# The upper levels of a block-triangular inverse: products of 128x128 against products of its 64x64 squares

## The chip, the cores and the metric

The kernel runs on one core of a Trainium2 chip. Its time is the device time of one execution, in microseconds (us). A core has TensorE for matrix products (PE in the profile, PEld for its weight loads), VectorE (DVE), ScalarE (ACT), GpSimd (POOL) and SyncE (SP, which issues the DMAs here). SBUF and PSUM have 128 partitions each; TensorE reads SBUF and writes PSUM.

## The reference, cut to what matters

Two blocks of a network work on 256 tokens of width 2048 in float32. The part in question is the gated delta rule of the second block. It runs for eight heads, in two directions, over chunks of 64 tokens:

```python
a_mat = m + jnp.eye(CHUNK)        # m: strictly lower triangular, one per head, direction and chunk
rhs = jnp.concatenate([v * beta, kb * jnp.exp(gc)[..., None]], axis=-1)
sol = lax.linalg.triangular_solve(a_mat, rhs, left_side=True, lower=True, unit_diagonal=True)
...
v_new = uc - jnp.einsum("bhck,bhkv->bhcv", wc, s)
o = jnp.einsum("bhck,bhkv->bhcv", qd, s) + jnp.einsum("bhij,bhjv->bhiv", qkc, v_new)
s = s * gl[..., None, None] + jnp.einsum("bhck,bhcv->bhkv", kd, v_new)
```

The kernel uses chunks of 128 instead of 64, which gives the same sequence of states, and forms the inverse of each 128x128 triangular matrix itself.

## The kernel before, in words

Everything beside the delta rule is mostly large linear layers. Their weights come in units of 128x1024 numbers: a DMA into one of four slots of `raw`, a rounded copy `w_hi` by ACT (L610 in this stage), the rest `w_lo` by POOL (L582), then sixteen matmuls by PE (`product`, L1941 and L1944). A slot is free again when PE has used its unit.

In the delta rule, PE works on one pair of heads at a time, `one_way` (way A below) and `other` (way B), over `PAIRS` = 4 pairs. Each pair's steps are written out by hand in one order for PE, one for ACT and one for DVE, with units of the gates' layer (`fill(n)`, 28 units a pair) put between them where PE would otherwise wait. Way A has PSUM banks `x_ps` and `y_ps` 0 and 1, way B banks 2 and 3. A way holds four matrices (two directions by two chunks), each 128x128, side by side on the free axis: `t` is the inverse so far, `u` its transpose, `m` the triangular matrix.

The inverse is built from diagonal blocks. DVE makes the inverses of the 16x16 blocks by substitution. Three levels then join neighbours: level 4 joins 16 to 32, level 5 joins 32 to 64, level 6 joins 64 to 128. After level 4 or 5, a matrix holds only the diagonal blocks of that size, so its two off-diagonal 64x64 squares are zeros until level 6. A level of a way takes these steps:

- PE, first product: `x_ps = m^T t` for the four matrices (L2385; at level 4 with the masked `mm4`).
- ACT copies `x_ps` to `x` in SBUF (`level` of ACT, L1007).
- PE, second product: `x_ps = u^T x` (L2391, levels 4 and 5 only) and `y_ps = x^T u` (L2392).
- DVE subtracts the result from `t` and `u` (L1732 at level 4, L1744 at level 5, L1751 at level 6, there only the one 64x64 square that is not zero).

PE's order in a level is: first product of A, first of B, second of A, second of B. No `fill` stands between the start of level 4 and the end of `first_solve` (L2398), which needs level 6's result. DVE has one other instruction among these, `group_out` between level 4 and level 5 (L1614, a reduction for the gates' layer). ACT's `fill(23)` (L610) stands right before its first copy. A float32 matmul of the program shows in the trace as two weight loads and two MATMUL records.

Of the kernel before, what the change touches and what calls it, by code (L numbers as in the profile page):

```python
# [20 lines left out]
ALU = mybir.AluOpType  # L21
# [4 lines left out]
P = 128  # L26
# [122 lines left out]
def four1(v):  # L149

    return v.rearrange("p (n i) -> p n i", n=4)


def flat(v):

    return v.rearrange("p d c h -> p (d c h)")
# [40 lines left out]
def build(nc, t, out):  # L197
    ctx = ExitStack()
    with ctx:
# [8 lines left out]
        def steps(name, names):  # L208
            return Steps(sem(name), names)

        def rounds(name, names):
# [117 lines left out]
        dn_dve = [steps(f"dn_dve{w}", ["one"] + [f"cv{y}{k}" for k in range(NT) for y in range(3)]  # L329
                        + ["rn", "rq", "qs", "ks", "dsub", "dmin", "m0", "m1", "m2", "m3", "qk", "blk", "mm4", "red", "dl", "r0", "r1"]  # L330
                        + [y for n in range(1, BASE) for y in (f"pr{n}", f"su{n}")] + ["cp", "ex0", "ex1", "t4", "u4"]
                        + [f"l5{n}" for n in range(4)] + ["u60", "u61", "vd0", "vd1", "v10", "v11", "ra", "rb", "v20", "v21",
                                                          "o", "orn", "on", "ot", "lo"]) for w in range(2)]
# [779 lines left out]
        def _(dve):  # L1113
# [102 lines left out]
            for i in range(4):  # L1216
# [6 lines left out]
                w = ROWS["even_w_dw"]  # L1223
# [409 lines left out]
            for p in range(PAIRS):  # L1633
                def from_pe(w, name):
                    dve.wait_ge(dn_pe[w.w].sem, dn_pe[w.w].at(name, p))
# [92 lines left out]

                def level4(w):
                    from_pe(w, "tu4")  # L1730
                    for part, bank in ((w.t, w.x_ps), (w.u, w.y_ps)):
                        nc.vector.tensor_tensor(part, part, four1(bank), ALU.subtract).then_inc(dn_dve[w.w].sem, 1)  # L1732

                def level5(w):

# [85 lines left out]
                for w in ways:  # L1821
                    level4(w)
# [11 lines left out]
            with dve.Fori(0, 4) as i:  # L1834
                for k in range(2):
# [9 lines left out]
                    fr, part = both[1][:, :, 1, :], scr[:, 2 + k].rearrange("p (m n) -> p m n", m=2)  # L1845
# [49 lines left out]
        def _(pe):  # L1895
# [113 lines left out]
            for q in range(TT):  # L2009
                for c in range(8):  # L2010
                    m = nc.tensor.transpose(ps[:, 2 * q + c // 4, (c % 4) * P:(c % 4 + 1) * P], z[:, Z_AGT + c, q * P:(q + 1) * P], ident[:])
            m.then_inc(ln_pe.sem, 1)
            for j in range(8):
                if j == 5:

                    pe.wait_ge(ln_dve.sem, ln_dve.at("n11"))
                    for c in range(8):
                        for q in range(TT):
                            m = nc.tensor.transpose(ps[:, c // 2, (c % 2) * T + q * P:(c % 2) * T + (q + 1) * P],
                                                    scr[:, 2 * q + c // 4, (c % 4) * P:(c % 4 + 1) * P], ident[:])  # L2020
# [69 lines left out]
            for name, width in (("cq", QL), ("kv", KVW)):  # L2090
                bank = 2 * (OG[name] % 2)
# [25 lines left out]
            for c in range(4):  # L2117
                for q in range(TT):
                    m = nc.tensor.transpose(ps[:, c // 2, (c % 2) * T + q * P:(c % 2) * T + (q + 1) * P], cqn[q][:, c * P:(c + 1) * P], ident[:])
            m.then_inc(od_pe.sem, 1)  # L2120
            pe.wait_ge(od_dve.sem, od_dve.at("kv1"))
            for c in range(2):
                for q in range(TT):
                    m = nc.tensor.transpose(ps[:, 2, c * T + q * P:c * T + (q + 1) * P], ckvn[q][:, c * P:(c + 1) * P], ident[:])
            m.then_inc(od_pe.sem, 1)
            for q in range(TT):
                m = nc.tensor.transpose(ps[:, 3, q * P:(q + 1) * P], ikn[:, q * P:(q + 1) * P], ident[:])
# [153 lines left out]
            for c in range(DC):  # L2281
                m = nc.tensor.matmul(ps[0:64, 0, :], sc_w[:, c].rearrange("p h n -> p (h n)"), a[:, c].rearrange("p s n -> p (s n)"), start=(c == 0), stop=(c == DC - 1))
# [10 lines left out]
            for q in range(TT):  # L2293
                for s in range(2):
                    m = nc.tensor.matmul(ps[:, 1, q * 32:q * 32 + 32], sc_feat[:, s * T + q * P:s * T + (q + 1) * P], pick,
                                         start=(s == 0), stop=(s == 1))
            m.then_inc(sc_pe.sem, 1)
            pe.wait_ge(group_free, IN2_G + 4)
            for g in range(FG):
                if g:  # L2300
                    pe.wait_ge(fo_act.sem, fo_act.at("ab", g - 1))
                for q in range(TT):
                    m = nc.tensor.matmul(ps[:, 2, q * T:(q + 1) * T], z[:, Z_F + g, q * P:(q + 1) * P], z[:, 40, :], start=True, stop=True)
# [5 lines left out]
                for q in range(TT):  # L2309
                    for s in range(2):  # L2310
                        m = nc.tensor.matmul(ps[:, 3, 0:T], z[:, 48 + q, s * P:(s + 1) * P], z[:, 41 + 2 * s + q, :],  # L2311
                                             start=(q == 0 and s == 0), stop=(q == 1 and s == 1))
# [3 lines left out]
                if g == 3:  # L2316
                    pe.wait_ge(sc_dve.sem, sc_dve.at("g1"))
                    for n in range(4):
                        d = n % 2
                        m = nc.tensor.matmul(ps[:, 0, 16 * n:16 * n + 16], tri[:, n, :], flat(dsc[:, GG])[:, 16 * d:16 * d + 16], start=True, stop=True)  # L2320
                    m.then_inc(sc_pe.sem, 1)
            blk = lambda v, n: v[:, n * P:(n + 1) * P]
            for p in range(PAIRS):
# [4 lines left out]
                def from_act(w, name):  # L2328
                    pe.wait_ge(dn_act[w.w].sem, dn_act[w.w].at(name, p))

                def from_dve(w, name):
                    pe.wait_ge(dn_dve[w.w].sem, dn_dve[w.w].at(name, p))
# [39 lines left out]
                def turn(w):  # L2372
# [2 lines left out]
                        m = nc.tensor.transpose(blk(w.y_ps, n), w.tu[:, at, :], ident[:])  # L2375
                    m.then_inc(dn_pe[w.w].sem, 1)

                def level(l, ready):
                    for w in ways:
                        if l == 4:  # L2380
                            from_act(w, "tt")
                        else:
                            from_dve(w, ready)
                        for n in range(4):
                            m = nc.tensor.matmul(blk(w.x_ps, n), (w.mm4 if l == 4 else w.m)[:, n, :], w.t[:, n, :], start=True, stop=True)  # L2385
                        m.then_inc(dn_pe[w.w].sem, 1)
                    for w in ways:
                        from_act(w, f"x{l}")
                        for n in range(4):
                            if l < 6:  # L2390
                                nc.tensor.matmul(blk(w.x_ps, n), w.u[:, n, :], w.x[:, n, :], start=True, stop=True)  # L2391
                            m = nc.tensor.matmul(blk(w.y_ps, n), w.x[:, n, :], w.u[:, n, :], start=True, stop=True)  # L2392
                        m.then_inc(dn_pe[w.w].sem, 1)

                def first_solve(w):
# [61 lines left out]
                for l, ready in ((4, None), (5, "u4"), (6, "l53")):  # L2457
                    level(l, ready)
# [79 lines left out]
```

## Time and profile before

| what | value |
|---|---|
| median of 3 runs | 2274.88 us (2274.41 to 2275.27) |
| profiled execution | 2274.89 us, span 2273.1 us |
| PE busy | 98% of the span |
| DVE, ACT, POOL busy | 45%, 46%, 75% |
| levels 4 to 6, each of the four pairs | 16.0 us of the span |

A busy share is the time in which an engine had at least one instruction under way. Matmuls are pipelined: one starts before the last has drained, so PE's pace is read from the starts of its rows, not from the length of one. In a timeline row, neighbouring instructions of one line and kind are merged, with their number behind the x.

### The profile page before, as it was taken

The numbers are of one execution on the slowest core, as the hardware profiler recorded it, in microseconds if no ns is written. First come the engines' busy times: TensorE is split into PE (matmuls) and PEld (weight loads), VectorE is DVE, ScalarE is ACT, GpSimd is POOL, SyncE is SP. The second block draws the span as 40 slices with busy tenths as digits, with TensorE's granted clock in tenths as the row PEclk, the third lists the DMA queues.
The fourth block names the chain that finished last, engine by engine and source line by source line (L and its number), as shares of the span: only waits on it lengthen the run. The fifth ranks groups of instructions, "written<-read, shape, count | busy, mean of one in ns | idle before, by whom it ended". The sixth has DMA issues, their size and how long they took to land.

```text
span 2273.1 us, 33387 instructions
## 1 busy us (share of the span) xinstructions
PE 2217.1 (98%) x12170; PEld 1909.5 (84%) x12170; DVE 1027.0 (45%) x1762; ACT 1036.3 (46%) x1442; POOL 1715.4 (75%) x721
## 2 busy tenths in 40 slices
PE   7999999999999999999999999999999999999998
PEld 6888888878888788888888888887888888888886
DVE  3991242025853141647473734405813822831841
ACT  5433455454566554535353535444333333333343
POOL 6888868867667975657474747897888888888885
PEclk9999999999999999999999999999999999999999
DMA  6666545646445654535353535665666656656654
GB/s 208 189 191 189 182 139 176 195 124 178 145 140 190 213 150 125 146 109 158 106 156 110 158 107 175 198 204 156 188 194 192 188 194 190 190 193 191 190 191 142
DMA packets 321435, 384.05 MB, mean 169 GB/s; under 512 B 14654, under 2 KB 255141, under 8 KB 321061
## 3 DMA queue, kind: packets, MB, share of 16 engines
q1 hardware_dynamic: 317237, 376.75, 54.8%
q10 hardware_dynamic: 4080, 5.64, 0.8%
q8 instruction: 85, 1.39, 0.3%
q14 instruction: 33, 0.27, 0.0%
HBM read 380.24 MB, written 2.10 MB: 168 GB/s over the span
## 4 chain that ended last, share of the span: by engine, by line
PE 92%; DVE 2%; issue 2%; ACT 2%; POOL 1%; DMA 1%; ACTq 0%; POOLq 0%; DVEq 0%
PE lin_ps L1941 35%; PE lin_ps L1944 17%; PE lin_ps L1982 9%; PE lin_ps L1980 9%; PE lin_ps L1981 9%; POOL w_lo L582 1%; PE ps L2392 1%; PE ps L1913 1%; PE ps L2385 1%; PE ps L2391 1%; PE ps L2311 1%; ACT w_hi L610 1%; PE ps L2243 0%; DMA raw<-in_odd_w_out 0%; PE lin_ps L2166 0%
## 5 line engine op out<-in xcount | busy, mean ns | idle before, releaser
L582 POOL TENSOR_TENSOR w_lo<-raw,w_hi 128x1024 fp32r<-128x1024 f32 x716 | 1715.1, 2403 | 538.6 <-ACT w_hi L610 440.4
L1941 PE MATMUL lin_ps<-a,w_hi 128*128 128x512 f32 x3200 | 1020.9, 400 | 0.9 <-POOL w_lo L582 0.8
L610 ACT ACTIVATE w_hi<-raw 128x1024 fp32r<-128x1024 f32 x456 | 479.2, 1059 | 568.8 <-PE lin_ps L1944 356.1
L1944 PEld LDWEIGHTS lin_ps<-a,w_lo 128*128 128x128 f32 x3200 | 601.9, 188 | 142.2
L1944 PE MATMUL lin_ps<-a,w_lo 128*128 128x256 f32 x3200 | 629.9, 278 | 0.0
L1941 PEld LDWEIGHTS lin_ps<-a,w_hi 128*128 128x128 f32 x3200 | 491.4, 189 | 8.5 <-issue 5.2
L621 ACT ACTIVATE w_hi<-raw 128x1024 fp32r<-128x1024 f32 x228 | 242.1, 1062 | 384.8 <-PE lin_ps L1944 225.6
L1980 PE MATMUL lin_ps<-w_hi,b 128*128 128x512 f32 x704 | 274.7, 390 | 1.6 <-POOL w_lo L582 1.5
L1981 PE MATMUL lin_ps<-w_lo,b 128*128 128x512 f32 x704 | 274.0, 389 | 0.0
L1982 PE MATMUL lin_ps<-w_hi,b 128*128 128x512 f32 x704 | 273.9, 389 | 0.0
L1980 PEld LDWEIGHTS lin_ps<-w_hi,b 128*128 128x128 f32 x704 | 132.1, 188 | 30.2 <-POOL w_lo L582 3.0
L1981 PEld LDWEIGHTS lin_ps<-w_lo,b 128*128 128x128 f32 x704 | 132.2, 188 | 27.3
L1982 PEld LDWEIGHTS lin_ps<-w_hi,b 128*128 128x128 f32 x704 | 132.1, 188 | 27.3
L1179 DVE SCALAR_TENSOR_TENSOR x<-x,lin_ps 128x512 f32<-128x512 f32 x32 | 20.6, 683 | 296.5 <-PE lin_ps L1982 296.5
L1941 PE MATMUL lin_ps<-b,w_hi 128*128 128x512 f32 x352 | 112.5, 401 | 2.9 <-POOL w_lo L582 2.2
L1980 PE MATMUL lin_ps<-w_hi,a 128*128 128x512 f32 x256 | 99.8, 390 | 0.0
L1982 PE MATMUL lin_ps<-w_hi,a 128*128 128x512 f32 x256 | 99.6, 389 | 0.0
L1981 PE MATMUL lin_ps<-w_lo,a 128*128 128x512 f32 x256 | 99.6, 389 | 0.0
L1880 DVE TENSOR_TENSOR b<-scr,b 128x512 f32 x32 | 92.4, 2889 | 4.7 <-DVE b L1878 0.5
L1876 DVE SCALAR_TENSOR_TENSOR scr<-scr 128x512 f32<-128x512 f32 x32 | 88.8, 2775 | 1.1
L1238 DVE SCALAR_TENSOR_TENSOR ps<-z,vec,ps 128x254 f32<-128x254 f32 (+28 forms) x232 | 88.2, 460 | 0.0
L1878 DVE CAST b<-scr 128x512 f32 x32 | 78.0, 2437 | 5.1 <-DVE scr L1876 5.1
(379 smaller groups left out, 2154.6 us busy)
## 6 DMA issues: line engine op xcount, KB each, us to landing
raw<-in_w_in SPq DMA_DIRECT2D x144, 512.0 KB, 3.7
raw<-in_w_mlp_up SPq DMA_DIRECT2D x128, 512.0 KB, 3.9
raw<-in_w_mlp_down SPq DMA_DIRECT2D x128, 512.0 KB, 3.6
raw<-in_even_w_in SPq DMA_DIRECT2D x112, 512.0 KB, 3.6
raw<-in_odd_w_in SPq DMA_DIRECT2D x40, 512.0 KB, 3.7
raw<-in_even_w_out SPq DMA_DIRECT2D x32, 512.0 KB, 4.2
raw<-in_odd_w_out SPq DMA_DIRECT2D x32, 512.0 KB, 4.6
raw<-in_w_o SPq DMA_DIRECT2D x32, 512.0 KB, 4.4
```

Source lines behind the costliest of these rows:

```text
L582: nc.gpsimd.tensor_tensor(w_lo[:, slot], raw[:, slot], w_hi[:, slot].bitcast(F32), ALU.subtract).then_inc(lo_done, 1)
L610: nc.scalar.activation(w_hi[:, slot], raw[:, slot], ACT.Copy).then_inc(hi_done, 1)
L621: nc.scalar.activation(w_hi[:, slot], raw[:, slot], ACT.Copy).then_inc(hi_done, 1)
L1238: nc.vector.scalar_tensor_tensor(out=acc[c][:, k:T], in0=u[c][:, 0:T - k], scalar=per_channel(w + 8 * (TAPS - 1 - k) + c), in1=acc[c][:, k:T],
L1876: nc.vector.scalar_tensor_tensor(out=tm2, in0=tmp, scalar=0.0, in1=tmp, op0=ALU.max, op1=ALU.mult).then_inc(ml_dve.sem, 1)
L1878: nc.vector.tensor_copy(bb[:, :, 0, :], tm2).then_inc(ml_dve.sem, 1)
L1880: nc.vector.tensor_tensor(bb[:, :, 1, :], tm2, bb[:, :, 0, :].bitcast(F32), ALU.subtract).then_inc(ml_dve.sem, 1)
L1941: nc.tensor.matmul(lin_ps[:, 2 * parity + m, :], hi[:, k, m * P:(m + 1) * P], src[:, kk].rearrange("p s n -> p (s n)"), start=(q == 0 and ...
L1944: last = nc.tensor.matmul(lin_ps[:, 2 * parity + m, 0:T], lo[:, k, m * P:(m + 1) * P], src[:, kk, 0, :], start=False, stop=(q == n - 1 and ...
L1980: nc.tensor.matmul(acc, ah, hi[:, k, :], start=(j == 0 and k == 0), stop=False)
L1981: nc.tensor.matmul(acc, ah, lo[:, k, :], start=False, stop=False)
L1982: last = nc.tensor.matmul(acc, al, hi[:, k, :], start=False, stop=(j == 7 and k == 1))
```

## The change

At levels 4 and 5 each product of two 128x128 matrices is written as two products of 64x64 squares, one on partitions 0 to 63 and one on 64 to 127, each writing its own square of PSUM. At level 6 each product is the one 64x64 square that is used: for the first two of the four matrices it goes from partitions 0 to 63 to partitions 64 to 127 in the first product, for the other two the other way round, and back in the second. The off-diagonal squares of levels 4 and 5 are no longer written, so DVE's subtraction of level 4 takes only the diagonal squares, as 64 partitions by 8 by 64, in two instructions as before. ACT's copies are as they were.

```diff
                 def level4(w):
                     from_pe(w, "tu4")
-                    for part, bank in ((w.t, w.x_ps), (w.u, w.y_ps)):
-                        nc.vector.tensor_tensor(part, part, four1(bank), ALU.subtract).then_inc(dn_dve[w.w].sem, 1)
+                    blocks = w.xy_ps.rearrange("p (m n) -> p m n", m=8)
+                    for rows in (slice(0, 64), slice(64, P)):
+                        nc.vector.tensor_tensor(w.tu[rows, :, rows], w.tu[rows, :, rows], blocks[rows, :, rows], ALU.subtract).then_inc(dn_dve[w.w].sem, 1)
...
+                def squares(l, n):
+
+                    halves = slice(0, 64), slice(64, P)
+                    return [(h, h) for h in halves] if l < 6 else [(halves[n // 2], halves[1 - n // 2])]
+
                 def level(l, ready):
                     for w in ways:
...
                         for n in range(4):
-                            m = nc.tensor.matmul(blk(w.x_ps, n), (w.mm4 if l == 4 else w.m)[:, n, :], w.t[:, n, :], start=True, stop=True)
+                            for k, o in squares(l, n):
+                                m = nc.tensor.matmul(w.x_ps[o, P * n + k.start:P * n + k.stop], (w.mm4 if l == 4 else w.m)[k, n, o], w.t[k, n, k],
+                                                     start=True, stop=True)
                         m.then_inc(dn_pe[w.w].sem, 1)
                     for w in ways:
                         from_act(w, f"x{l}")
                         for n in range(4):
                             if l < 6:
-                                nc.tensor.matmul(blk(w.x_ps, n), w.u[:, n, :], w.x[:, n, :], start=True, stop=True)
-                            m = nc.tensor.matmul(blk(w.y_ps, n), w.x[:, n, :], w.u[:, n, :], start=True, stop=True)
+                                for k, o in squares(l, n):
+                                    nc.tensor.matmul(w.x_ps[k, P * n + k.start:P * n + k.stop], w.u[k, n, k], w.x[k, n, k], start=True, stop=True)
+                            for k, o in squares(l, n):
+                                m = nc.tensor.matmul(w.y_ps[k, P * n + o.start:P * n + o.stop], w.x[o, n, k], w.u[o, n, o], start=True, stop=True)
                         m.then_inc(dn_pe[w.w].sem, 1)
```

PE before, first pair, level 4: the first products of way A (tiles in `z`) and way B (`scr`), then the second products of way A. The numbers behind the names are partitions by columns of the moving operand, as the program writes it.

```order
L2385 MATMUL ps<-z 128x128 x4
L2385 MATMUL ps<-scr,z 128x128 x4
L2391 MATMUL ps<-z 128x128
L2392 MATMUL ps<-z 128x128
L2391 MATMUL ps<-z 128x128
L2392 MATMUL ps<-z 128x128
```

The same place in the changed kernel, whose lines 2392, 2400 and 2402 are these three matmuls.

```order
L2392 MATMUL ps<-z 64x64 x8
L2392 MATMUL ps<-scr,z 64x64 x8
L2400 MATMUL ps<-z 64x64 x2
L2402 MATMUL ps<-z 64x64 x2
L2400 MATMUL ps<-z 64x64 x2
L2402 MATMUL ps<-z 64x64 x2
```

Each matmul has become two of half the edge, in the same place between the waits; a way's level goes from 12 matmuls to 24 at levels 4 and 5.

PE before, first pair, level 6 (first products of A and B, then the second ones).

```order
L2385 MATMUL ps<-z 128x128 x4
L2385 MATMUL ps<-scr 128x128 x4
L2392 MATMUL ps<-z 128x128 x4
L2392 MATMUL ps<-scr 128x128 x4
```

The same place in the changed kernel.

```order
L2392 MATMUL ps<-z 64x64 x4
L2392 MATMUL ps<-scr 64x64 x4
L2402 MATMUL ps<-z 64x64 x4
L2402 MATMUL ps<-scr 64x64 x4
```

Here the number stays, and only the size goes down. On DVE two instructions of 64x8x64 a way stand where two of 128x512 stood, and nothing else moves on any engine.

## Rows read from the trace of the kernel before

**Rows 1.** The page, busy time and instructions of each engine

```profile
PE 2217.1 (98%) x12170; PEld 1909.5 (84%) x12170; DVE 1027.0 (45%) x1762; ACT 1036.3 (46%) x1442; POOL 1715.4 (75%) x721
```

**Rows 2.** Windows, levels of pairs 1 and 4: PE, PEld, DVE, ACT, POOL; clock, DMA

```profile
986.80:1002.80 16.00, 15.09 (x131) 14.61 (x129) 6.54 (x15) 4.53 (x7) 3.43 (x2) 1.00 0.29 86
...
1320.90:1336.90 16.00, 15.09 (x131) 14.61 (x130) 6.54 (x15) 4.53 (x7) 3.42 (x2) 1.00 0.28 82
```

**Rows 3.** Timeline of PE, first pair: start, us, line, shapes, number [idle before]

```profile
986.83 1.06 PE L2385 MATMUL ps<-z 128*128 128x128 f32 x8
987.72 1.06 PE L2385 MATMUL ps<-scr,z 128*128 128x128 f32 x8
988.68 0.49 PE L2391 MATMUL ps<-z 128*128 128x128 f32 x2
...
992.36 1.06 PE L2385 MATMUL ps<-z 128*128 128x128 f32 x8
993.90 1.16 PE L2385 MATMUL ps<-scr 128*128 128x128 f32 x8 [0.48 <-DVE scr L1732]
...
998.46 1.06 PE L2385 MATMUL ps<-z 128*128 128x128 f32 x8
999.95 1.16 PE L2385 MATMUL ps<-scr 128*128 128x128 f32 x8 [0.43 <-DVE scr L1744]
...
1002.79 0.62 PE L2398 MATMUL ps<-z 128*128 128x128 f32 x4
1003.65 0.71 PE L2398 MATMUL ps<-z,scr 128*128 128x128 f32 x4 [0.24 <-DVE scr L1751]
```

**Rows 4.** Timeline of ACT, same stretch

```profile
987.08 1.06 ACT L610 ACTIVATE w_hi<-raw 128x1024 fp32r<-128x1024 f32 x1 [1.25 <-PE lin_ps L1944]
988.05 0.58 ACT L1007 ACTIVATE z<-ps 128x512 f32<-128x512 f32 x1
...
993.45 0.60 ACT L1007 ACTIVATE z<-ps 128x512 f32<-128x512 f32 x1 [4.04 <-PE ps L2385]
```

**Rows 5.** Timeline of DVE, same stretch

```profile
992.56 1.28 DVE L1732 TENSOR_TENSOR scr<-scr,ps 128x512 f32<-128x512 f32 x2 [0.50 <-PE ps L2392]
993.76 1.22 DVE L1614 TENSOR_REDUCE z<-lin_ps 128x512 f32<-128x1024 f32 x1
...
998.67 1.23 DVE L1744 TENSOR_TENSOR scr<-scr,ps 32x128 f32<-32x128 f32 x4 [0.56 <-PE ps L2392]
1002.04 0.60 DVE L1751 TENSOR_TENSOR z<-z,ps 64x128 f32<-64x128 f32 x2 [2.14 <-PE ps L2392]
```

**Rows 6.** Timeline of POOL, its first instruction after the same stretch

```profile
1008.47 2.40 POOL L582 TENSOR_TENSOR w_lo<-raw,w_hi 128x1024 fp32r<-128x1024 f32 x1 [17.90 <-ACT w_hi L610]
```

**Rows 7.** Timeline of PE, indexer of the first block, operands on 64 partitions

```profile
545.40 0.39 PE L1944 MATMUL lin_ps<-b,w_lo 128*128 128x256 f32 x2
545.72 0.93 PE L2196 MATMUL ps<-own,z 64*128 64x128 f32 x8
546.58 0.50 PE L1941 MATMUL lin_ps<-b,w_hi 128*128 128x512 f32 x1
...
549.56 0.39 PE L2196 MATMUL ps<-own,z 64*128 64x128 f32 x2
```

**Rows 8.** The line of these matmuls: ns of one, min/median/max, and shapes

```profile
L2196 PE MATMUL ps<-own,z x64: 272/374/378, 541.0 to 569.3; 64*128 64x128 f32 x32, 64*128 64x256 f32 x32
```

**Rows 9.** A line that loads weights of 64 columns: ns of one, min/median/max

```profile
L2282 PEld LDWEIGHTS ps<-a,b x16: 133/134/135, 849.7 to 853.1; 128*64 128x64 f32 x16
```

**Rows 10.** Timeline of PEld, eight weight loads before matmuls of only 16 columns

```profile
890.08 0.98 PEld L2320 LDWEIGHTS ps<-dsc,tri 128*128 128x128 f32 x8
```

**Rows 11.** Windows around PE's idle stretches of 1.05 and 2.17 us

```profile
737.90:741.40 3.50, 2.45 (x12) 1.70 (x10) 0.00 (x0) 1.47 (x2) 2.38 (x1) 1.00 1.11 362
...
1377.80:1381.20 3.40, 1.34 (x7) 1.16 (x8) 2.62 (x3) 2.74 (x4) 3.40 (x2) 1.00 0.01 2
1381.30:1384.60 3.30, 3.30 (x13) 2.82 (x12) 0.69 (x1) 0.42 (x2) 3.30 (x3) 0.50 0.80 241
```

## The prediction

> **What bounds the kernel now.** I read the page first: PE is busy for 98% of the span, no other engine for more than 75% [rows 1], so time is only won where PE's own instructions go or PE's waits shrink. Then the windows of the four stretches in which levels 4 to 6 run: the reader is to see that each is 16 us long with PE busy for 15.1, DVE for 6.5, ACT for 4.5, and that the first and the last pair agree to the hundredth, at a granted clock of 1.00 (2.4 GHz) [rows 2]. I can work out one pair and take it four times. The timeline of PE in the first pair shows the levels as almost one closed run from 986.83 to the start of `first_solve` at 1002.79, broken by two waits for DVE, 0.48 and 0.43 us, and a third of 0.24 before way B's solve at 1003.65 [rows 3]. So this stretch is bound by PE, with DVE close behind. POOL has filled all slots and idles for 17.9 us across it [rows 6]; weights are not what comes late when the stretch shrinks by a few us.
>
> **The pace of a pass.** Each float32 matmul is two records; I call one a pass. Eight passes of 128x128 start at 986.83 and the next eight at 987.72 [rows 3]: 0.89 / 8 = 0.111 us, with a little more in the longer runs, 0.1117. A pass could be paced by its 128 columns or by its weights. The loads before matmuls of only 16 columns say that weights alone set the same pace: eight loads in 0.98 us of which the last one's 0.19 is its own, so 0.79 / 7 = 0.113 [rows 10]. Hence both must halve for a pass to halve. A load of 64 columns takes 134 ns [rows 9] against about 190, 0.056 less, so loads do halve; and passes of 256 and 128 columns differ by 378 - 272 = 106 ns [rows 8], so 64 columns fewer are worth about 0.053. A 64x64 pass should therefore follow the last in its tile after about 0.056 us.
>
> **The sum if the two tiles do not overlap.** Levels 4 and 5 have 2 ways x 12 matmuls x 2 = 48 passes each; they become 96 at 0.056, 5.38 against 5.36 us. Nothing is won there. Only level 6 gains: its 32 passes stay 32 and cost 0.056 less each, 1.8 us of PE, of which the chain below lets through about 1.0.
>
> **Whether they overlap.** Squares on partitions 0 to 63 and 64 to 127 lie in different rows and different columns of the array. The trace has a neighbour, the indexer, whose operands take 64 partitions, two passes of 128 and two of 256 columns for the lower half, and the same for the upper half behind them. One after the other they would need 4 x 0.111 + 4 x 0.216 = 1.31 us. They start at 545.72 and PE's next matmul starts at 546.58 [rows 7], 0.86, and 0.65 is what one half needs by itself. In the other instance two of 0.37 us [rows 8] lie within 0.39 us together [rows 7], 0.02 apart at most. So the two halves do run beside each other, also when the second half is issued four passes later. The same rows show a price for going from 128 to 64 partitions: the last full pass starts at 545.40 + 0.39 - 0.28 = 545.51 and the next should start 0.11 later, at 545.62, but starts at 545.72. I take 0.09 us once a pair; the way back falls into a wait.
>
> What these rows don't show is two halves that write the same PSUM bank: the indexer gives each its own bank, and the change puts both squares of a matrix into one bank, on different partitions. The Trainium skill, "TensorEngine Tiling (Array Packing)", Restrictions and Gotchas, says that different row tiles cannot access the same PSUM bank at once. Taken to the letter it would bring the sum without overlap, 2271 us; taken as a rule about the same partitions of a bank it leaves the overlap whole. No row here decides.
>
> So the pace of a pass, over both tiles, lies between 0.028 (full overlap) and 0.112 (a pass costs what it does now). I take 0.029, nearest to the indexer's rows.
>
> **The sum with overlap, first pair.** Delays: the last product's stream to ACT 0.2 (992.36 + 0.89 = 993.25 to 993.45 [rows 3, 4]), ACT's copy 0.60 [rows 4], the stream to DVE 0.3 at most, DVE 1.28, 1.23 and 0.60 for levels 4, 5 and 6 [rows 5], and 0.05 from ACT or DVE back to PE (993.84 to 993.90 [rows 5, 3]). DVE's new subtraction at level 4 has 8 x 64 = 512 elements a partition as before, so 1.28 stays; its bounds are that and, if the strided form were to cost the 1.22 of a reduction over twice as many [rows 5] for each instruction, 1.2 more a way. A first product of 16 passes takes 0.46, a second one of 32 takes 0.93; at level 6 I leave the overlap out, since four passes of one tile follow each other before the other's, and take 8 x 0.056 = 0.45.
>
> Level 4: A 986.92 to 987.38, B to 987.84. ACT is held by the unit's copy until 988.14, so A's copy ends at 988.63 as before [rows 4] and the second products start at 988.68 as before [rows 3]: nothing of the 0.9 us saved on the first products comes through. A to 989.61, B to 990.54. DVE takes A from 989.91 to 991.19, B to 992.47, then the reduction of 1.22 [rows 5].
> Level 5: A's first product 991.24, B's 992.52 to 992.98 (both wait for DVE), second products to 993.91 and 994.84. DVE takes A from 994.21 to 995.44, B to 996.67; the reduction between is over by 993.7.
> Level 6: A 995.49, B 996.72 to 997.17, A's second to 997.62, B's waits for its copy (997.97) and runs 998.02 to 998.47. DVE 997.92 to 998.52, and B 998.77 to 999.37.
> `first_solve` of A starts at 998.57 instead of 1002.79, of B at 999.42 instead of 1003.65 [rows 3]: 4.2 us a pair. PE's work has fallen by more (5.4 at levels 4 and 5, 1.8 at level 6); the rest turns into waits for DVE and one for ACT. What comes next on all engines is triggered by `first_solve` and by units that stand ready, so it moves as a whole. Four pairs: 16.9 us. From the profiled execution, 2274.89 us (span 2273.1 and 1.8 around it, the median of the runs being 2274.88), that gives **2258.0 us**. With level 6 overlapping too it is some 1.5 less, with paces of 0.032 or DVE a little slower some 2 more: 2255.5 to 2262 is this case's own range.
>
> **The rivals.**
> *One after the other.* The hardware keeps the two squares apart, for the shared bank or another reason. Then levels 4 and 5 stay, level 6 gives 1.0, the change of mode takes 0.1: 0.9 a pair, 3.6 in all, and 1.5 less if a pass takes 0.058. 2271 to 2273 us, no change by the bound of 0.2%, 4.5 us, below which a measurement can't tell it from none. For it: no shared bank in the rows. Against it: rows 7.
> *Half overlap.* Each pair of instructions hinders the other somewhat, pace 0.035 to 0.045: 2262 to 2268.
> *Too many short instructions.* This ends on the slow side. PE now gets a load and a matmul every 0.112 us, one instruction in 0.056. Full overlap asks for four in 0.056. If what feeds PE were at its limit today, a pass would stay at 0.112: 96 more passes a pair at levels 4 and 5, 10.7 us, less the 0.9 of waits that vanish, plus 0.1, so 9.9 a pair and 2314. It decides from where 192 passes cost 0.9 us more than their 10.7 now, a pace of 0.060; at 0.070 it is 2282. Against it: the four instructions of two passes within some 0.02 us [rows 7], though those may have been queued up, and the weights as the better reason for 0.112 [rows 10].
> The Trainium skill, "TensorE: Matmul & The Clock Gate", Part 1, gives about 62 ns per MATMUL where its sequencer decodes in software and about 25 ns between starts as a floor otherwise. By the first figure the change would cost about 0.3 a pair, 2276 us; by the second the full overlap just fits. Starts 0.02 apart [rows 7] speak against the first.
> *The clock.* With the gain, PE waits about a third of each level. After an idle stretch of 2.17 us, in a window with PE busy for 1.34 of 3.4, the granted clock fell to 0.50 (1.2 GHz) for the next 3.3; with 2.45 busy of 3.5 it stayed at 1.00 [rows 11]. My levels have about 2.8 busy of 4 with waits under 0.9, nearer to the latter. If it fell once a pair for 3.4 us, half of that is lost, 1.7 x 4 = 7: 2265.
>
> **Chances.** Full overlap 0.57, half 0.12, one after the other 0.16, too many instructions 0.10, clock 0.05. Faster by over 0.2% (under 2270.3) has the first two and most of the last, with a little taken off for sums that stop short: 0.72; within 0.2% 0.17; slower 0.11. The range goes from 2255.5, the foot of the first case, to 2275, which takes in the serial one.
>
> **What would show it.** In the timeline of PE after, the first product of way A should span about 0.5 us for 16 passes and the second about 0.9 for 32, with waits for DVE of about 0.7 before way A's and 0.8 before way B's first product at level 5, and one of about 0.8 before the second products of level 4. `first_solve` should come about 11.7 us after the first matmul of level 4, not 16. Starts of the two tiles' matmuls should pair up. If the second products still take 1.8 us, the tiles don't overlap, and my forecast is wrong by 13 us; if they take over 2, the feed is the bound. The granted clock must stay at 1.00 in the four stretches, and DVE's subtraction at level 4 must stay at 1.28 us a way.

## The result, and the profile after

| | before | changed |
|---|---|---|
| median | 2274.64 us (4 runs) | 2259.83 us (2258.28 to 2261.01, 4 runs) |
| span of the profiled execution | 2273.1 us | 2257.6 us |

The ratio is 0.9937, 95% interval 0.9924 to 0.995: faster by 0.5 to 0.8%, 14.3 us at the middle. The forecast was 2258.0.

The page of the changed kernel: the busy shares and TensorE's clock, as [rows 1] of before.

```profile
PE 2192.3 (97%) x12554; PEld 1882.7 (83%) x12554; DVE 1026.1 (45%) x1762; ACT 1036.1 (46%) x1442; POOL 1717.2 (76%) x721
...
PEclk9999999999999999999999999999999999999999
```

PE has 384 MATMUL records more and 25 us less busy time. The slices of the clock look unchanged; they are too coarse, as the next view shows. Windows of the changed kernel: the levels of the first and the third pair (the counterpart of [rows 2]), and in each the end of level 6 and what follows. The columns are again PE, PEld, DVE, ACT, POOL, granted clock, DMA.

```profile
984.70:996.30 11.60, 8.04 (x225) 7.15 (x224) 6.81 (x15) 4.42 (x7) 3.33 (x2) 1.00 0.39 116
992.80:996.20 3.40, 1.78 (x44) 1.37 (x38) 2.29 (x9) 1.19 (x2) 0.00 (x0) 1.00 0.00 0
996.30:999.60 3.30, 3.30 (x17) 3.10 (x14) 2.60 (x9) 0.00 (x0) 0.00 (x0) 0.50 0.00 0
1201.50:1213.10 11.60, 8.04 (x225) 7.15 (x224) 6.81 (x15) 4.42 (x7) 3.36 (x2) 1.00 0.40 113
1213.20:1216.50 3.30, 3.23 (x21) 2.77 (x21) 2.97 (x10) 0.00 (x0) 0.00 (x0) 1.00 0.00 0
```

The levels take 11.60 us instead of 15.96, with 3.56 of them idle on PE. Behind the first pair's levels the granted clock is at 0.50, behind the third's at 1.00: in 3.3 us PE ran 17 matmul records in the one and 21 in the other.

Timeline of PE in the first pair, the counterpart of [rows 3]; lines 2392, 2400, 2402 and 2408 are before's 2385, 2391, 2392 and 2398.

```profile
984.70 0.68 PE L2392 MATMUL ps<-z 64*64 64x64 f32 x16
985.22 0.63 PE L2392 MATMUL ps<-scr,z 64*64 64x64 f32 x16
986.47 0.33 PE L2400 MATMUL ps<-z 64*64 64x64 f32 x4 [0.61 <-ACT z L1007]
986.63 0.28 PE L2402 MATMUL ps<-z 64*64 64x64 f32 x4
986.75 0.28 PE L2400 MATMUL ps<-z 64*64 64x64 f32 x4
...
987.33 0.28 PE L2402 MATMUL ps<-z 64*64 64x64 f32 x4
...
989.12 0.68 PE L2392 MATMUL ps<-z 64*64 64x64 f32 x16 [0.57 <-DVE z L1733]
990.55 0.68 PE L2392 MATMUL ps<-scr 64*64 64x64 f32 x16 [0.75 <-DVE scr L1733]
...
993.50 0.46 PE L2392 MATMUL ps<-z 64*64 64x64 f32 x8 [0.40 <-DVE z L1745]
994.76 0.46 PE L2392 MATMUL ps<-scr 64*64 64x64 f32 x8 [0.81 <-DVE scr L1745]
995.05 0.45 PE L2402 MATMUL ps<-z 64*64 64x64 f32 x8
995.92 0.45 PE L2402 MATMUL ps<-scr 64*64 64x64 f32 x8 [0.42 <-ACT scr L1007]
996.30 1.22 PE L2408 MATMUL ps<-z 128*128 128x128 f32 x4
```

Four passes start every 0.117 us (six times from 986.63 to 987.33), 0.029 a pass, and four passes lie within 0.28 us together. Six waits have come, for DVE and for ACT, 3.56 us in all. DVE and ACT in the same stretch, for [rows 5] and [rows 4]:

```profile
987.66 1.40 DVE L1733 TENSOR_TENSOR z<-z,ps 64x512 f32<-64x512 f32 x2 [10.96 <-PE ps L2402]
989.10 1.40 DVE L1733 TENSOR_TENSOR scr<-scr,ps 64x512 f32<-64x512 f32 x2
```

```profile
984.87 1.06 ACT L610 ACTIVATE w_hi<-raw 128x1024 fp32r<-128x1024 f32 x1 [1.25 <-PE lin_ps L1945]
985.83 0.58 ACT L1007 ACTIVATE z<-ps 128x512 f32<-128x512 f32 x1
```

DVE's subtraction takes 1.40 us a way, not 1.28. ACT's copy of way A starts only when the unit's copy is through, as before.

The bill: per pair the levels give 15.96 - 11.60 = 4.36, four times 17.4 us. Against it stand the clock's falls, each from 1.00 to 0.50 for about 3.4 us. From `first_solve` to the next pair's level 4 it is 95.41 us behind pair 3 (1213.13 to 1308.54), where the clock held, and 96.63 and 97.00 behind pairs 1 and 2; from the last pair's to the end of PE's wait of 2.16 us behind the delta rule it is 44.30, where the kernel before has 42.98. That is 1.2, 1.6 and 1.3, together 4.1. 17.4 - 4.1 = 13.3 is what the stretch from the first level 4 to that wait has lost (393.03 to 379.74). The other 2.1 of the two profiles' difference lies ahead of it, where nothing was changed: the first level 4 starts at 986.83 before and at 984.70 after. In the ten traces of this case it starts between 983.77 and 986.83, and that of the kernel before is the latest; 1.0 us of the 2.1 is there at the first DMA that PE waits for (11.76 against 10.77). So the change itself is worth about 13 us, and part of the measured 14.3 is this spread.

### The profile page after: what moved, and what is told of

Its sections match the earlier page's. It is cut to its first block, busy times and chain, and to the rows that moved or that the text cites. A ratio compares the mean times of both kernels' runs of the same rounds, so it can differ in the third digit from the quotient of the medians.

```text
span 2257.6 us, 34155 instructions
## 1 busy us (share of the span) xinstructions
PE 2192.3 (97%) x12554; PEld 1882.7 (83%) x12554; DVE 1026.1 (45%) x1762; ACT 1036.1 (46%) x1442; POOL 1717.2 (76%) x721
## 3 DMA queue, kind: packets, MB, share of 16 engines
q8 instruction: 88, 1.44, 0.3%
## 4 chain that ended last, share of the span: by engine, by line
PE 92%; DVE 2%; ACT 2%; issue 2%; POOL 1%; DMA 1%; ACTq 0%; POOLq 0%; DVEq 0%
PE lin_ps L1942 36%; PE lin_ps L1945 18%; PE lin_ps L1982 9%; PE lin_ps L1983 9%; PE lin_ps L1981 9%; POOL w_lo L582 1%; PE ps L1914 1%; PE ps L2312 1%; ACT w_hi L610 1%; DMA raw<-in_odd_w_out 0%; PE ps L2244 0%; PE lin_ps L2106 0%; PE lin_ps L2107 0%; PE lin_ps L2108 0%; PE lin_ps L2167 0%
```

## The experiments

Eight kernels ran, in two groups, each group on one chip with its own runs of the kernel before (medians 2273.97 and 2272.65 us). The changed kernel did not run in these groups: it is compared by the ratios, and by the length of a stretch in the two traces.

**level6_only.** Squares at level 6 alone; DVE's subtraction of level 4 is that of the kernel before (its lines are left out here).

```diff
...
-                    return [(h, h) for h in halves] if l < 6 else [(halves[n // 2], halves[1 - n // 2])]
+                    return [(slice(0, P), slice(0, P))] if l < 6 else [(halves[n // 2], halves[1 - n // 2])]
```

> Squares of 64 at level 6 alone; levels 4 and 5 and DVE's subtraction of level 4 as in the kernel before. Theory (the two tiles overlap also where four passes of one tile stand before four of the other, 0.24 us a product instead of 0.89): first_solve 1.4 us earlier a pair, 5.6 in all, 2269 us, no clock drop. Rival (level 6's products run one tile after the other, 0.45 us a product): 1.0 a pair, 2271.

Measured: 2272.23 us, ratio 0.9991 (0.9981 to 1.0). Timeline of PE at level 6, first pair, and the windows before and after `first_solve`:

```profile
997.92 0.45 PE L2391 MATMUL ps<-z 64*64 64x64 f32 x8
999.31 0.45 PE L2391 MATMUL ps<-scr 64*64 64x64 f32 x8 [0.94 <-DVE scr L1744]
999.60 0.45 PE L2401 MATMUL ps<-z 64*64 64x64 f32 x8
1000.47 0.46 PE L2401 MATMUL ps<-scr 64*64 64x64 f32 x8 [0.42 <-ACT scr L1007]
1000.85 0.71 PE L2407 MATMUL ps<-z 128*128 128x128 f32 x4
```

```profile
998.00:1001.40 3.40, 2.04 (x36) 1.68 (x36) 2.09 (x8) 1.20 (x2) 0.00 (x0) 1.00 0.00 0
1001.50:1004.70 3.20, 3.13 (x11) 2.77 (x11) 2.57 (x9) 0.00 (x0) 0.00 (x0) 0.50 0.02 5
```

The levels shrank by 1.30 us a pair (986.18 to 1000.85 is 14.67), near the 1.4 expected, and eight passes start within 0.45 - 0.22 = 0.23 us (0.22 is the last one's own length; one after the other in one tile they would need 7 x 0.058 = 0.41), so they overlap although four of one tile stand before four of the other. But the time was missed by 3 us: the clock fell behind two of the four pairs, the first and the third. To the next level 4 it is 96.82 and 96.87 us behind these and 95.31 behind the second, so about 3 of the 5.2 us won went back.

**level45_only.** Squares at levels 4 and 5 alone.

```diff
-                    return [(h, h) for h in halves] if l < 6 else [(halves[n // 2], halves[1 - n // 2])]
+                    return [(h, h) for h in halves] if l < 6 else [(slice(0, P), slice(0, P))]
```

> Squares at levels 4 and 5 alone, level 6 with products of 128x128. Theory: levels 4 and 5 give the larger part, about 3.1 us a pair, so first_solve is 1.1 us later a pair than in the changed kernel; PE waits less at level 6, so the granted clock should stay at 1.00 there, which gives back about 4 us: 2260 to 2262. Rival (the clock falls whatever level 6 does): 2264 to 2265.

Measured: 2259.33 us, ratio 0.9936 (0.9921 to 0.9952), the changed kernel's own time. The levels take 12.89 us, 1.29 more a pair, and the clock fell behind none of the four: from `first_solve` on, every pair is alike, 95.48 us. From the first level 4 to the end of PE's wait behind the delta rule it takes 380.99 us, the changed kernel 379.74: of the 5.2 us that level 6 gives in the full change, the falls took back all but 1.3. That the times are equal to the half us has another part. Behind that wait the changed kernel's clock falls once more (0.50 from 1364.90 to 1368.30) and here it holds (1.00 from 1365.30 to 1368.60), though PE was busy for 1.28 and 1.29 us of the 3.40 before it. After such a stretch the clock sometimes falls and sometimes doesn't; what decides is not shown.

**one_tile.** Both squares the lower one; the upper ones are left out, so that the result is not the inverse.

```diff
-                    return [(h, h) for h in halves] if l < 6 else [(halves[n // 2], halves[1 - n // 2])]
+                    return [(halves[0], halves[0])] * 2 if l < 6 else [(halves[0], halves[1])]
```

> The same number and sizes of matmuls as in the changed kernel, but both squares of a product are the lower one (partitions 0 to 63), so nothing can overlap; the upper squares are not computed. Theory (the gain of levels 4 and 5 is the overlap of two tiles): a pass of 64x64 follows the last after 0.056 us, a first product takes 0.9 and a second one 1.8, and the time is 2271 to 2273. Rival (short passes are simply cheaper, or DVE's form is what helps): as the changed kernel, 2260. Rival (what feeds PE is a bound): over 0.06 a pass, 2276 or more.

Measured: 2289.34 us, ratio 1.0065 (1.005 to 1.008): slower. Timeline of PE, first pair, and two windows of it:

```profile
983.77 1.14 PE L2392 MATMUL ps<-z 64*64 64x64 f32 x16
984.75 1.09 PE L2392 MATMUL ps<-scr,z 64*64 64x64 f32 x16
985.69 0.39 PE L2400 MATMUL ps<-z 64*64 64x64 f32 x4
985.92 0.39 PE L2402 MATMUL ps<-z 64*64 64x64 f32 x4
...
989.42 1.09 PE L2392 MATMUL ps<-z 64*64 64x64 f32 x16
...
994.23 0.63 PE L2400 MATMUL ps<-z 64*64 64x64 f32 x4
994.66 0.63 PE L2402 MATMUL ps<-z 64*64 64x64 f32 x4
```

```profile
983.80:992.40 8.60, 8.04 (x135) 7.90 (x135) 3.96 (x5) 2.95 (x5) 3.28 (x2) 1.00 0.50 152
992.50:1002.90 10.40, 9.37 (x93) 8.88 (x90) 2.84 (x10) 1.54 (x3) 0.00 (x0) 0.50 0.01 2
```

At the full clock four passes take 0.23 us, 0.058 each, and level 4 takes 5.65 us (983.77 to 989.42) where the kernel before has 5.53: without overlap nothing is won, as the serial sum said, and 0.029 in the changed kernel is the overlap of two tiles. But the time is 17 us above what that sum allowed, because the clock then fell to half in the middle of every pair's levels for 13.7 us. PE was busy for 8.04 of the 8.60 us before that, the same share as in the kernel before (15.09 of 16.00 [rows 2]), but on a quarter of the array. The busy share alone doesn't tell whether the clock holds. That the one tile is the reason is likely and not shown: the numbers multiplied differ as well.

**busy_waits.** Matmuls of no use in three of the waits, one in each level.

```diff
...
+                def idle(l, w):
+                    for n in range(4) if l < 6 else (0, 0, 1, 1, 2, 2, 3, 3):
+                        for k, o in squares(l, n):
+                            nc.tensor.matmul(w.y_ps[k, P * n + o.start:P * n + o.stop], w.m[o, n, k], w.t[o, n, o], start=True, stop=True)
...
+                        if l > 4 and w is ways[0]:
+                            idle(l, w)
+                    if l == 4:
+                        idle(l, ways[0])
...
```

> The changed kernel with eight matmuls of 64x64 more (0.46 us) in each of three of PE's waits of a pair (before the second products of level 4, before way B's first product of levels 5 and 6), into squares that the next product overwrites. Theory (the clock falls behind three of four pairs because PE is idle too much in level 6, and each fall costs 1.3 us): the granted clock stays at 1.00 in all four pairs and the time falls by up to 4 us, to 2256, though 96 matmuls were added. Rival (the fall has nothing to do with these waits): three falls stay and the time stays at 2260 or goes up by some tenths.

Measured: 2255.42 us, ratio 0.9918 (0.9904 to 0.9931). Windows, first pair: its levels, the end of level 6, and what follows.

```profile
985.20:996.80 11.60, 9.73 (x274) 8.84 (x273) 6.80 (x15) 4.42 (x7) 3.29 (x2) 1.00 0.39 112
993.30:996.70 3.40, 2.53 (x58) 2.12 (x53) 2.27 (x8) 1.20 (x2) 0.00 (x0) 1.00 0.00 0
996.80:1000.10 3.30, 3.23 (x22) 2.78 (x21) 2.97 (x10) 0.00 (x0) 0.00 (x0) 1.00 0.02 5
```

The levels still take 11.60 us, PE is busy for 1.7 of them more, the clock holds behind all four pairs, and every pair takes the same 107.00 us, level 4 to level 4, where the changed kernel has 108.23, 108.60 and 107.01. From the first level 4 to the end of PE's wait behind the delta rule it takes 375.52 us, 4.2 less than the changed kernel, and the falls had cost 4.1. (The intervals of the two ratios overlap a little, so the gain rests on this stretch.)

The mean granted clock is on record for every timed run, and one fall of 3.4 us to half takes 0.0008 from it. It is 0.994 in all five runs here, 0.994 or 0.995 in the four of level45_only, 0.991 in three of the changed kernel's and 0.993 in the fourth, and 0.992 in all ten of level6_only. So the traces are no exceptions. Three experiments together put the cause in PE's idle time in level 6: without that level's squares no fall comes (level45_only), with them alone some do (level6_only), and with them and work in the waits none (busy_waits). Why the clock holds behind some pairs and falls behind others whose levels are as long to 0.01 us is open.

**copy_first.** ACT's copy of the unit behind its copies of level 4.

```diff
-                fill(23)
                 for l in (4, 5, 6):
                     for w in ways:
                         level(w, f"x{l}")
+                    if l == 4:
+                        fill(23)
```

> The changed kernel with ACT's copy of a unit (the fill of 23) moved from before its copies of level 4 to behind them. Theory (nothing of the 0.9 us saved on level 4's first products comes through, because ACT is held by that copy): way A's second product of level 4 starts 0.4 us earlier after the first matmul, and first_solve comes 0.4 earlier a pair, 11.2 us instead of 11.6; 2258 if the clock falls as often. Rival (the wait is bound by the first product itself or by the latency to ACT): 11.6 stays.

Measured: 2256.26 us (2251.82 to 2260.1), ratio 0.9925 (0.9908 to 0.9942). The wait of 0.61 us went down to 0.23 and the levels to 11.22 (PE, first pair):

```profile
985.17 0.68 PE L2393 MATMUL ps<-z 64*64 64x64 f32 x16
985.69 0.63 PE L2393 MATMUL ps<-scr,z 64*64 64x64 f32 x16
986.55 0.33 PE L2401 MATMUL ps<-z 64*64 64x64 f32 x4 [0.23 <-ACT z L1007]
```

ACT's order had been in the way. In the profiled run the clock fell behind two pairs; the runs spread over 8 us, against 1.6 in busy_waits. Falls that come in some runs and not in others are part of the spread: the mean granted clock is 0.994 in the fastest run (2251.82 us), 0.993 in the next (2255.45) and 0.992 in the other two (2257.07 and 2260.1). Four falls at 1.2 to 1.6 us are some 6 us, so they are not all of it.

**old_subtraction.** DVE's level 4 in the form of the kernel before.

```diff
-                    for rows in (slice(0, 64), slice(64, P)):
-                        nc.vector.tensor_tensor(w.tu[rows, :, rows], w.tu[rows, :, rows], blocks[rows, :, rows], ALU.subtract).then_inc(dn_dve[w.w].sem, 1)
+                    for part, bank in ((w.t, w.x_ps), (w.u, w.y_ps)):
+                        nc.vector.tensor_tensor(part, part, four1(bank), ALU.subtract).then_inc(dn_dve[w.w].sem, 1)
```

> The changed kernel with DVE's two instructions of 128x512 at level 4 as in the kernel before; the off-diagonal squares of t and u are then not zero, but nothing that is timed depends on their values. Theory (64 partitions by 8 blocks of 64 cost 1.40 us a way against 1.28): first_solve 0.1 to 0.25 us earlier a pair, under 1 us in all, 2259. Rival (DVE's subtraction is off the path): no change of the 11.60 us between level 4's first matmul and first_solve.

Measured: 2258.04 us (2254.32 to 2260.34), ratio 0.9934 (0.9917 to 0.9951). The levels take 11.25 us instead of 11.60 in three pairs, 0.35 less and more than I expected; in the second it is 11.36, where the clock fell just before `first_solve`. DVE, first pair:

```profile
986.81 1.29 DVE L1732 TENSOR_TENSOR z<-z,ps 128x512 f32<-128x512 f32 x2 [10.95 <-PE ps L2401]
988.01 1.28 DVE L1732 TENSOR_TENSOR scr<-scr,ps 128x512 f32<-128x512 f32 x2
```

Way B's pair starts 1.20 us behind way A's, against 1.44 in the changed kernel. DVE's subtraction is on the path. In the time this is under the spread (granted clock 0.993 in the fastest run, 0.992 in the others).

**quarters.** A unit in four parts in PE's waits. `plan` maps level, product (0 the first, 1 the second) and way to a unit and its part; the lines that issue a part are left out here.

```diff
...
+                plan = {(4, 1, 0): [(20, 0)], (5, 0, 0): [(20, 1)], (5, 0, 1): [(20, 2)], (6, 0, 1): [(20, 3)]}
...
-                for step, n in ((first_solve, 20), (states, 21), (from_state, 22), (second_solve, 23)):
+                for step, n in ((first_solve, 21), (states, 22), (from_state, 23), (second_solve, 24)):
...
```

> The changed kernel with the unit that stood behind first_solve cut in four parts of 0.70 us, each in one of PE's waits (before the second products of level 4, before both first products of level 5, before way B's of level 6); the units behind move up by one. Theory (the waits of 0.61, 0.57, 0.75 and 0.81 us are free for other work at a price of two changes of tile size, about 0.09 each, and the clock then stays at 1.00): the level takes 0.8 us a pair more, but holds 2.8 us of work, so 2.0 a pair is won, and 4 us by the clock: 2248. Rival (the changes of size and late products give it back): 2256, no better than with matmuls of no use in the waits.

Measured: 2247.78 us (2247.07 to 2248.12), ratio 0.9890 (0.9874 to 0.9907). PE at level 5, first pair, and the window of the levels:

```profile
989.42 0.73 PE L1943 MATMUL lin_ps<-a,w_hi 128*128 128x512 f32 x2
989.99 0.40 PE L1946 MATMUL lin_ps<-a,w_lo 128*128 128x256 f32 x2
990.32 0.68 PE L2404 MATMUL ps<-z 64*64 64x64 f32 x16
990.93 0.73 PE L1943 MATMUL lin_ps<-a,w_hi 128*128 128x512 f32 x2
991.50 0.40 PE L1946 MATMUL lin_ps<-a,w_lo 128*128 128x256 f32 x2
991.83 0.68 PE L2404 MATMUL ps<-scr 64*64 64x64 f32 x16
```

```profile
985.40:997.60 12.20, 11.38 (x242) 9.86 (x241) 6.80 (x15) 4.87 (x8) 3.37 (x2) 1.00 0.38 111
```

A part holds the place of a wait for 0.90 us (989.42 to 990.32). The levels take 12.16 us, 0.56 more, and hold a unit; PE idles for 0.8 of them instead of 3.6. A pair takes 104.8 us, level 4 to level 4, and the clock holds. It beats the kernel before by 1.1% and the changed one too.

**quarters_copy_first.** Both, with other places for the parts.

```diff
...
+                plan = {(5, 0, 0): [(20, 0)], (5, 0, 1): [(20, 1)], (6, 0, 1): [(20, 2)], (6, 1, 1): [(20, 3)]}
...
```

> The same with ACT's copy moved as in copy_first and the parts put before both first products of level 5, before way B's first and before way B's second of level 6. Theory: level 4's wait is gone by itself, the fourth part overshoots a wait of 0.42 by 0.5 us, and together it comes out 0.2 to 0.4 us a pair before quarters: 2247. Rival (the wait of level 4 was the better place for the fourth part): 2249 or more.

Measured: 2247.3 us (2246.53 to 2247.99), ratio 0.9889 (0.9872 to 0.9905). A pair takes 104.6 us instead of 104.8, at the lower end of what was expected; 0.7 us from the first level 4 to the wait behind the delta rule, which the timed runs can't tell from quarters.

## Why the prediction was right, and where not

**The pace and the overlap.** Right. 0.029 a pass was forecast and is measured; two squares in one PSUM bank, on different partitions, do not hinder each other. Of the Trainium skill's rule on row tiles and one bank ("TensorEngine Tiling (Array Packing)", Restrictions and Gotchas), the reading that ties it to shared partitions is the one that these traces bear out. The serial sum was right as well: one_tile's level 4 at the full clock is within 0.12 us of the kernel before.

**The chain by hand.** `first_solve` was to come 998.57 - 986.92 = 11.65 us after the first matmul, and comes after 11.60. The waits were to be about 0.8, 0.7 and 0.8 at levels 4 and 5 and 0.8 for way B at level 6; the rows have 0.61, 0.57, 0.75 and 0.81. A row counts a wait from the modelled end of the last matmul, later than the pace does, so starts are the better test. The second products of level 4 start 1.77 us after the first matmul (986.47 - 984.70), and 1.76 was forecast: the wait was sized right, and copy_first shows that ACT's unit copy set it, as the chain had it. Level 5 then comes late, 4.42 instead of 4.32 us after the first matmul for way A and 5.85 instead of 5.60 for way B, because DVE's subtraction was put at 1.28 and costs 1.40. Level 6 makes up for it: its products were put at 0.45 and take 0.23 to 0.29, because I left out of the sum the overlap where four passes of a tile stand together, which the indexer's rows had already shown [rows 7] (the range had it). That the two cancel to 0.05 us is luck. One figure beside the sum was wrong: PE's work at levels 4 and 5 falls by 10.7 - 5.6 = 5.1 or 5.2 us at the pace of 0.029, not 5.4.

**The rival of too many instructions.** Excluded: PE took four instructions, two loads and two matmuls, in 0.058 us for 64 in a row.

**The clock.** This step failed. I gave it 0.05, on the ground that the levels had 2.8 us busy of 4, nearer to the row where the clock held. That was read from level 4. My own chain had four products of 0.45 us at level 6, 1.8 us busy between 994.84 and 998.57. Level 6, where the matmuls are fewest and the waits longest, has 1.78 of 3.40, between my two rows (1.34 of 3.40, where it fell, and 2.45 of 3.50, where it held [rows 11]). The busy share was not the whole of it either, as one_tile shows. The clock fell behind three pairs of four. Its price was forecast as 1.7 a fall and measured as 1.2 to 1.6. So the levels gave 17.4 us where 16.9 were forecast, and the clock took 4.1 of it, which leaves 13.3. The time came out within 2 us of the forecast partly by luck: the stretch ahead of the levels, which the change does not touch, gave 2.1 us in the profiled runs. That a fall would not come was wrong.

## What to carry to other kernels

Cutting block-diagonal products into squares paid here only through the overlap of tiles at levels 4 and 5: one square after the other cost what the whole did (5.65 us for level 4 against 5.53). When the cut makes a stretch that PE bound into one that a chain of engines binds, work out the idle time of each stretch behind it, not of the whole, and put pieces of independent work in there at once; here that added 11 us, by the ratios, to the 14 of the change itself, and the clock held behind all four pairs. Two changes that each look right (level 6's squares here) can all but cancel through the clock, so run them apart. And compare a stretch in the traces before believing 2 us in the time: the part that nobody touched differed by as much.

## What the runs showed of the hardware that I had not expected

- The granted clock fell to 0.50 in the middle of a stretch in which PE was busy for 8.04 of 8.60 us, when all its matmuls used one 64x64 tile (one_tile); with two tiles in turn and PE busy for 8.04 of 11.60 us it held until the end of level 6.
- The same wait of 2.16 to 2.18 us, with PE busy for 1.28 to 1.31 of the 3.40 us up to it, was followed by a granted clock of 0.50 in the changed kernel and of 1.00 in level45_only and busy_waits.
- Two DVE instructions on different halves of the partitions, 512 elements a partition each, take 1.40 us together where two on all 128 partitions take 1.28, though one alone takes the same 0.68 to 0.69 in either form.
- The PE overlaps two tiles also when four passes of one stand in front of four of the other: eight passes in 0.23 us (level6_only).
